# Chunked-attention scores computed as 64x64 pieces in the four quarters of the matmul array

## What is computed

```
kb = jnp.concatenate([shift(kc, j) for j in reversed(range(A_WIN_CHUNKS))], axis=2)   # A_WIN_CHUNKS = 2
logits = jnp.einsum('bnqkgd,bnskd->bnkgqs', qc, kb).astype(jnp.float32) * (d ** -0.5)
logits = logits - sl[None, None, :, :, None, None] * dist       # |qpos - kpos|, the same in every chunk
m = jnp.maximum(jnp.max(logits, axis=-1, keepdims=True), sink)
p = jnp.exp(logits - m)
probs = p / (jnp.sum(p, axis=-1, keepdims=True) + jnp.exp(sink - m))
```

## Time and profile before

| | |
|---|---|
| runs (3) | median 717.54 us, 717.44 to 718.22 |
| profiled execution | 717.69 us, of which the span from its first to its last instruction is 715.9 us |
| busy | TensorE 99%, weight loads 82%, VectorE 60%, ScalarE 44%, GpSimd 32% |
| granted TensorE clock, mean | 0.998 of full |
| DMA | 52.5 MB, a quarter of the 16 engines' time |

### The profile page before, as it was taken

The page is one execution under the profiler, slowest core; times in us unless marked ns, Lnnn a source line. Parts: engine busy times, 40 slices in busy tenths (PEclk is TensorE's granted clock), DMA queues, the critical chain, the costliest instruction groups (busy, mean ns, idle before and its releaser), DMA issues.

```text
span 715.9 us, 11698 instructions
## 1 busy us (share of the span) xinstructions
PE 706.1 (99%) x3885; PEld 589.5 (82%) x3885; DVE 426.2 (60%) x930; ACT 311.7 (44%) x721; POOL 231.6 (32%) x204
## 2 busy tenths in 40 slices
PE   8999999999999999999999999999999999999996
PEld 8988888888888888888888888888888887888885
DVE  6785256776754677775467777636676786322231
ACT  6752444445533445464334636434454554112210
POOL 5723132143433214343231434232234542222200
PEclk9999999999999999999999999999999999999999
DMA  9921211020052101105211110521130275514211
GB/s 298 299 60 31 58 39 51 1 59 2 1 153 53 36 23 31 28 0 147 59 29 30 29 29 0 147 60 30 30 122 2 63 238 181 155 59 125 81 53 42
DMA packets 79144, 52.53 MB, mean 73 GB/s; under 512 B 36080, under 2 KB 71936, under 8 KB 79104
## 3 DMA queue, kind: packets, MB, share of 16 engines
q1 hardware_dynamic: 79104, 52.06, 25.4%
HBM read 43.14 MB, written 8.91 MB: 73 GB/s over the span
## 4 chain that ended last, share of the span: by engine, by line
PE 94%; DVE 4%; ACT 1%; issue 1%; DVEq 0%; POOL 0%; ACTq 0%; POOLq 0%
PE acc L1462 18%; PE acc L1464 18%; PE acc L1463 17%; PE score L1462 4%; PE score L1463 3%; PE score L1464 3%; PE score L1656 3%; PE trans L1463 3%; PE trans L1464 3%; PE trans L1462 3%; PE score L1658 3%; PE trans L1677 2%; PE score L1734 2%; PE mixo L1462 2%; PE mixo L1463 2%; PE mixo L1464 2%
## 5 line engine op out<-in xcount | busy, mean ns | idle before, releaser
L1462 PE MATMUL acc<-x_hi,w_hi 128*128 128x512 f32 x544 | 217.5, 400 | 0.0
L1464 PE MATMUL acc<-x_hi,w_lo 128*128 128x512 f32 x544 | 213.8, 393 | 0.0
L1463 PE MATMUL acc<-x_lo,w_hi 128*128 128x512 f32 x544 | 212.5, 391 | 0.0
L905 POOL TENSOR_TENSOR w_lo<-w_raw,w_hi 128x512 fp32r<-128x512 f32 x66 | 85.7, 1319 | 173.3 <-ACT w_hi L592 154.6
L1464 PEld LDWEIGHTS acc<-x_hi,w_lo 128*128 128x128 f32 x544 | 102.1, 188 | 23.2
L1462 PEld LDWEIGHTS acc<-x_hi,w_hi 128*128 128x128 f32 x544 | 102.2, 188 | 20.1 <-issue 1.8
L1463 PEld LDWEIGHTS acc<-x_lo,w_hi 128*128 128x128 f32 x544 | 102.3, 188 | 19.1
L761 ACT ACTIVATE logits<-logits,stats_b 128x256 f32<-128x256 f32 (+3 forms) x64 | 52.6, 824 | 46.6 <-DVE stats_b L1267 46.6
L1259 DVE CUSTOM_DVE_ANT_0 logits<-score,b_bias 128x512 f32<-128x512 f32 (+1 forms) x96 | 53.5, 598 | 22.3 <-PE score L1658 18.6
L770 ACT ACTIVATE p_hi<-trans 128x512 fp32r<-128x512 f32 x56 | 32.6, 596 | 63.4 <-PE trans L1677 39.4
L1286 DVE TENSOR_TENSOR p_lo<-trans,p_hi 128x512 fp32r<-128x512 f32 x56 | 38.0, 689 | 29.4 <-ACT p_hi L770 29.0
(11 more groups left out here) (248 smaller groups left out, 1369.1 us busy)
## 6 DMA issues: line engine op xcount, KB each, us to landing
w_raw<-in_w_in SPq DMA_DIRECT2D x68, 256.0 KB, 3.4
mixed<-gates SPq DMA_DIRECT2D x9, 512.0 KB, 4.2
mix_raw<-mixed SPq DMA_DIRECT2D x8, 576.0 KB, 5.6
wo_raw<-in_w_out SPq DMA_DIRECT2D x8, 512.0 KB, 6.7
x_res<-in_x SPq DMA_DIRECT2D x8, 512.0 KB, 3.3
out_y<-y_row SPq DMA_DIRECT2D x16, 256.0 KB, 2.0
logits<-in_x SPq DMA_DIRECT2D x4, 512.0 KB, 8.1
wo_raw<-in_w_out SPq DMA_DIRECT2D x6, 256.0 KB, 5.7
```

Source lines behind the costliest of these rows:

```text
L905: last = pool.tensor_tensor(w_lo[:, slot, cols], w_raw[:, slot, cols], w_hi[:, slot, cols].bitcast(F32), ALU.subtract)
L1462: pe.matmul(out, a_hi, b_hi, start=start, stop=False, skip_group_check=True)
L1463: pe.matmul(out, a_hi, b_lo, start=False, stop=False, skip_group_check=True)
L1464: return pe.matmul(out, a_lo, b_hi, start=False, stop=stop, skip_group_check=True)
```

## The change

The scores of a step are computed in 64x64 pieces: for each i, each half c of 64 queries and each g one matmul with 64 queries as weights and only their own 128 keys as moving operand. Half c writes partitions c * 64 to c * 64 + 63 of the bank, columns 0 to 127 of tile i's part. So eight matmuls stand where four stood, and a piece uses one quarter of the array (rows by g, columns by c). VectorE then finds every query's window in the same columns and adds the bias for 128 partitions in one operation. A `nop` that isn't merged with its neighbours stands ahead of the matmuls.

```diff
--- before.py, VectorE
-                        for c in range(2):
-                            ps = slice(c * CHUNK, (c + 1) * CHUNK)
-                            bias = a_bias[ps, g, 0:2, :] if m == 0 else \
-                                a_bias[ps, g, 1:2, :].broadcast_to([CHUNK, 2, P])
-                            last = dve.tensor_tensor(a_band[ps, 2 * g:2 * g + 2, :], s[ps, :, c * CHUNK:c * CHUNK + P],
-                                                     bias, ALU.add)
-                        last.then_inc(s_free_dve, 1)
+                        bias = a_bias[:, g, 0:2, :] if m == 0 else a_bias[:, g, 1:2, :].broadcast_to([P, 2, P])
+                        dve.tensor_tensor(a_band[:, 2 * g:2 * g + 2, :], s[:, :, 0:P], bias, ALU.add)\
+                           .then_inc(s_free_dve, 1)
--- before.py, TensorE
                     outs = [s_bank(("a", m, g)) for g in range(2)]
+                    pe.nop(nofuse=True)
                     for i in range(2):
-                        t = 2 * m + i
-                        for g in range(2):
-                            ps = slice(g * DK, (g + 1) * DK)
-                            last = pe.matmul(outs[g][:, i * MEM:i * MEM + 3 * CHUNK], a_q[ps, t * P:(t + 1) * P],
-                                             a_k[ps, t * P:t * P + 3 * CHUNK], start=True, stop=True,
-                                             skip_group_check=True)
-                            if i == 1:
-                                last.then_inc(s_full, 1)
+                        for c in range(2):
+                            q0 = (2 * m + i) * P + c * CHUNK
+                            for g in range(2):
+                                ps = slice(g * DK, (g + 1) * DK)
+                                last = pe.matmul(outs[g][c * CHUNK:(c + 1) * CHUNK, i * MEM:i * MEM + P],
+                                                 a_q[ps, q0:q0 + CHUNK], a_k[ps, q0:q0 + P], start=True, stop=True,
+                                                 skip_group_check=True)
+                                if i == 1 and c == 1:
+                                    last.then_inc(s_full, 1)
```

## The result

The changed kernel takes 724.9 us (median of 4 runs, 724.16 to 725.63) against 717.61 us: 1.0101 times as long, with an interval of 1.0089 to 1.0114. It is slower by 7.3 us, where 4.0 us faster was forecast.

A forecast was written before the change was run, and what follows sets the result against it. TensorE was taken to bound the kernel: 717.69 us less 4.2 for sixteen shorter steps, plus 0.2 for starting four and 0.1 for bank and instruction supply, gave 713.8, as a median 713.6 us; range 712.6 to 716.8.

The forecast's parts named there:

- What bounds the kernel: In the loop TensorE is busy all the time at full clock, so its time is paid in full and VectorE's is hidden.
- what a step costs: Each of sixteen a_scores steps on TensorE falls from 0.85 to 0.59 us, 4.2 us saved in all.
- quarters run at once: In a_scores, row and column splits combine, so four records run together, in four groups; chance 0.68 with nearly all arriving.
- the allowance for starting four: Starting four records instead of two in a_scores may take a hundredth of a microsecond a step, 0.2 us in all.
- The rule against the change: Weight loads for a_scores' second column half would wait on the same rows: 1.36 us a step, 8 us more; small chance.
- The other edits: Halving VectorE's additions from 64 to 32 and adding the `nop` on TensorE's sequencer: both counted as zero.
- the supply of instructions: At (6, 0, 0), 32 matmul records follow in 1.2 us; late supply, together with the bank, 0 to 1 us, middle 0.1.
- the bank's signal: At (6, 0, 0) a_spread(1) needs a bank from VectorE, still 0.22 us late enough; at most 1.0 us in four turns.
- VectorE's part counted as zero: The 13.5 us of VectorE additions saved gain nothing, as TensorE doesn't wait for VectorE in the loop.
- What is late next: At (6, 0, 0), a_spread(1) would still find its bank free 0.22 us ahead; its transposes start without a wait.
- a serial array: Rival: in a_scores the column halves take turns once rows are split, 1.03 us a step, 720.4 us; chance 0.10.
- an array that stops at each step: Rival: exposed weight loads in a_scores, or a `nop` holding the array each time, 723 to 726 us; chance 0.04.

The follow-up runs named there:

- e9: The changed kernel with 128 already satisfied semaphore waits on TensorE ahead of its loop, four behind each of 32 products: 714.64 us, 0.9958 of the kernel before.
- e14: The changed kernel with TensorE's loop written out, no padding, and VectorE's additions in four operations of 64x256: 712.96 us, 0.9939 of the kernel before.
- e15: The changed kernel with four VectorE additions and 128 satisfied waits ahead of the loop, spread two behind each of 64 memory-projection products: 713.92 us, 0.9944 of before.
- e11: As e9, the changed kernel with 128 satisfied waits ahead of the loop, but VectorE adds the bias in four operations of 64x256: 714.19 us, 0.9953 of before.
- e4: The changed kernel with TensorE's loop written out, four turns in a row without a branch: 714.84 us, 0.9956 of the kernel before.
- e12: The kernel before with 15 satisfied waits ahead of each a_scores, 1621 instructions a turn: 727.26 us, 1.0146 of the kernel before.
- e7: The kernel before with 64 satisfied waits on TensorE ahead of its unchanged loop: 728.63 us, 1.0157 of the kernel before.
- e13: The kernel before with TensorE's loop written out: 716.74 us, 0.9987 of the kernel before.

## Why the prediction was wrong, point by point

- **What bounds the kernel, what a step costs, that quarters run at once.** Right. 0.25 us is saved in a step against 0.26 forecast, groups of four instead of pairs, 16 steps: 4.0 us against 4.0 after the allowance for starting four. With the instruction loads out of the way e9, e14 and e15 show it as time: two turns are 126.47 and 126.39 us in e9 instead of 127.4.
- **The rule against the change.** The Trainium skill, TensorE: Matmul & The Clock Gate, Part 3, "The mechanism", says that a weight load overlaps running matmuls only in another row group. The trace disagrees for column halves: by that rule the step would take 1.36 us and it takes 0.60, and groups that start 0.11 us apart, with 0.107 of it streaming, leave no room for a load that shows. Giving it a small chance was right.
- **The other edits: the step that failed.** "The `nop` is work of TensorE's sequencer" and the supply of instructions were weighed only as a rate at one place, (6, 0, 0), at "0 to 1 us for both". That 64 instructions more in a turn must also be kept, and what happens at the branch back if they aren't, did not come up; the whole term, with the bank's signal, stood at 0.1 us in the sum, and what happened at the two branches is worth 10.9 us. The profile before had it in view: 17 loads of instructions in queue 8, none of them in the second and third turn, a loop of 1561 instructions that just stayed.

  The Trainium skill, Runtime: NRT & Kernel Launch, "Instruction fetch mechanics", says that TensorE has room for 2048 instructions, filled in blocks of 16 KiB or 256 instructions, and that a taken branch out of the current window of two pages has to wait until its target is fetched. The trace agrees with the wait (3.3 us) and with the block: 16 KB a load, 254 instructions from load to load. It disagrees with a window of two: the kernel before branches back over 1561 instructions without a load. And 1628 is below 2048 and still lost its start. If blocks have 256 instructions, the runs say that a turn stays while it spans no more than seven of them. An estimate from that page's 2048 and 256 would be eight blocks of room, seven for the turn and one loaded ahead.
- **VectorE's part counted as zero.** Not worth anything in time, as forecast. That the wait of 0.35 us comes with two additions and not with four was not forecast; e11, with four, is 0.45 us faster than e9, where its forecast allowed 0.2, with overlapping intervals. e4 and e14 differ by 1.9 us, of which that wait is one part and a wait for split output weights of 1.1 us in e4's profiled tail another. The ratios' intervals overlap, and why VectorE starts later there was not tested.
- **What is late next.** a_spread(1) never waits in the changed kernel: right.
- **The range.** It reached to 716.8 and the slower rivals were a serial array or an array that stops at each step. The sign was lost to a mechanism outside the steps that I priced.

What stays open: why e12's second turn loads one block fewer than its neighbours' and so has no stop behind it, and where exactly the edge lies for this start of the loop, between 1593 instructions (no stop) and 1621 (one); and whether the late start of VectorE with two additions comes from its own instruction loads. That eight blocks is the size of the memory is worked out from the loads, not measured by itself.

## What to carry to other kernels

An edit that makes a loop's body longer is to be priced at the branch too: look at the times of the instruction loads in the profile before. If they are missing in the later turns, the body is being kept, and how near it is to losing its start decides; here 67 instructions more cost 11 us in two branches, and so did 64 that did nothing, ahead of the loop. The remedy is to move the loop's start in its block (e15) or to write the loop out where one engine's body no longer fits (e14); and to a stop like these add what the slow clock takes behind it (1.6 and 2.7 us behind 3.3 here).

## What the runs showed of the hardware

- Four quarter matmuls of 64x64 with different rows and columns start within 0.02 us of each other and run together: 16 records of 128 columns, each column passed twice, in 0.60 us.
- A taken branch to instructions that have to be loaded stopped TensorE for 3.3 us; with the clock at the 1.2 GHz level afterwards it cost 4.9 and 6.0 us. e7 and e12 stopped for up to 3.5 and 3.6 us.
- A loop of TensorE was kept, with no load in its second and third turn, where its first turn took six loads of 16 KB, and not kept where it took seven (14 kernels). What stood ahead of the loop decided as much as its length: with 64 instructions more ahead of the loop 1561 instructions were lost, with 128 more 1628 were kept.
- Written-out code loaded its instructions 29 and 30 times in e13 and e14 and never stopped for it (0.9987 and 0.9939 of the time before).
